# Moving one tile's gated sum from VectorE to GpSimd in the second joint block of a transformer kernel

## The reference

```python
for i in range(DEPTH):                      # DEPTH = 2
    h = _modulate(_rmsnorm(x, g_attn[i]), sh_a, sc_a)
    hc = _modulate(_rmsnorm(xc, g_attn[i]), shc_a, scc_a)
    q, k, v = _split_qkv(h, w_qkv[i])
    qc, kc, vc = _split_qkv(hc, w_qkv[i])
    ...                                     # joint attention, w_o, gates
    y = _hier_moe(tokens, ...)              # two experts of 32 per token, weighted sum
    x = x + gt_f * y[:b * n].reshape(b, n, d)
    if not last:
        xc = xc + gtc_f * y[b * n:].reshape(xc.shape)
```

## Time and profile before

| | us |
|---|---|
| median of 3 runs | 2367.75 |
| the runs | 2365.62, 2367.75, 2369.81 |
| profiled execution, device time | 2365.99 |
| its span in the trace | 2364.2 |
| busy: PE / DVE / ACT / POOL | 2154.2 / 1110.1 / 688.3 / 199.9 |

### The profile page before, as it was taken

How to read it: one execution, slowest core, us unless ns; L and a number is a source line. 1 busy time by engine, 2 the same in 40 slices (tenths; PEclk the granted TensorE clock), 3 DMA queues, 4 the chain that set the end, 5 groups by cost and what they waited for, 6 DMA issues and landing times.

```text
span 2364.2 us, 28723 instructions
## 1 busy us (share of the span) xinstructions
PE 2154.2 (91%) x11290; PEld 1348.1 (57%) x11290; DVE 1110.1 (47%) x1761; ACT 688.3 (29%) x1100; POOL 199.9 (8%) x304
## 2 busy tenths in 40 slices
PE   7999999998899999988988888888789999999996
PEld 5778788876787888865833233333466533333332
DVE  6677655465676556568531111111687422222223
ACT  4243344345234443257211111111337111111110
POOL 2000000010000000100111111011120000000000
PEclk9989999999899999999879899899999899999998
DMA  9745576573755656520779999999850699999995
GB/s 304 267 146 187 194 246 205 171 266 138 245 186 187 224 173 227 180 49 6 293 292 419 426 427 427 427 427 425 327 157 21 240 413 427 427 427 428 428 427 232
DMA packets 174936, 657.04 MB, mean 278 GB/s; under 512 B 15991, under 2 KB 61639, under 8 KB 149472
## 3 DMA queue, kind: packets, MB, share of 16 engines
q1 hardware_dynamic: 159216, 622.65, 68.1%
q0 software_dynamic: 13776, 29.99, 3.8%
q10 hardware_dynamic: 1824, 2.73, 0.3%
HBM read 649.97 MB, written 23.79 MB: 285 GB/s over the span
## 4 chain that ended last, share of the span: by engine, by line
PE 59%; DMA 21%; DVE 13%; ACT 4%; issue 1%; POOL 1%; SPq 1%; ACTq 0%; POOLq 0%; DVEq 0%
PE bank L737 30%; DMA sb_ring<-in_w_up 16%; PE bank L1374 11%; PE bank L1399 5%; DMA sb_arena<-in_w_up 3%; DVE sb_ring_rounded L2024 2%; PE bank L1332 2%; PE bank L751 2%; ACT sb_hb L1615 1%; PE bank L773 1%; DVE sb_st L2228 1%; PE bank L1385 1%; PE bank L926 1%; ACT sb_ring_rounded L1510 1%; PE bank L940 1%
## 5 line engine op out<-in xcount | busy, mean ns | idle before, releaser
L737 PE MATMUL bank<-sb_ring_rounded,sb_hT_rounded 128*128 128x512 f32 x2432 | 603.3, 397 | 22.8 <-DVE sb_ring_rounded L2024 9.7
L737 PEld LDWEIGHTS bank<-sb_ring_rounded,sb_hT_rounded 128*128 128x128 f32 x2432 | 457.9, 190 | 122.2 <-issue 12.6
L1374 PE MATMUL bank<-sb_ring,sb_arena 128*64 128x512 f32 x1568 | 436.7, 638 | 72.7 <-DMA sb_ring<-in_w_up 64.7
L2024 DVE TENSOR_TENSOR sb_ring_rounded<-sb_ring,sb_ring_rounded 128x2048 fp32r<-128x2048 f32 (+1 forms) x142 | 315.1, 2260 | 109.3 <-ACT sb_ring_rounded L1510 104.8
L737 PE MATMUL bank<-sb_ring_rounded,sb_arena_rounded 128*128 128x512 f32 x1408 | 356.4, 395 | 8.2 <-DVE sb_arena_rounded L2011 7.6
L1510 ACT ACTIVATE sb_ring_rounded<-sb_ring 128x2048 fp32r<-128x2048 f32 x146 | 268.1, 1887 | 125.6 <-PE bank L737 100.7
L1374 PEld LDWEIGHTS bank<-sb_ring,sb_arena 128*64 128x64 f32 x1568 | 132.4, 146 | 300.3 <-issue 296.0
L737 PEld LDWEIGHTS bank<-sb_ring_rounded,sb_arena_rounded 128*128 128x128 f32 x1408 | 265.8, 190 | 63.6 <-DVE sb_arena_rounded L2011 7.9
L1907 ACT ACTIVATE sb_hb<-bank 64x512 f32<-64x512 f32 x64 | 37.8, 590 | 688.9 <-PE bank L1374 688.9
L1399 PE MATMUL bank<-sb_ring,sb_arena 128*64 128x512 f32 x768 | 174.8, 597 | 2.5 <-DVE sb_arena L2857 2.5
L2857 DVE COPY sb_arena<-bank 128x256 f32<-128x256 f32 x64 | 27.1, 424 | 310.6 <-PE bank L1385 310.5
(11 more groups left out here) (376 smaller groups left out, 2259.4 us busy)
## 6 DMA issues: line engine op xcount, KB each, us to landing
sb_ring<-in_w_gate SPq DMA_DIRECT2D x50, 2048.0 KB, 30.2
sb_ring<-in_w_up SPq DMA_DIRECT2D x48, 2048.0 KB, 30.6
sb_ring<-in_w_down SPq DMA_DIRECT2D x48, 2048.0 KB, 25.6
sb_ring<-in_w_ada SPq DMA_DIRECT2D x48, 1024.0 KB, 7.4
sb_ring<-in_ffn_w_gu SPq DMA_DIRECT2D x44, 1024.0 KB, 7.7
sb_ring<-in_xa_w_kv SPq DMA_DIRECT2D x16, 1024.0 KB, 7.4
sb_ring<-in_ffn_w_down SPq DMA_DIRECT2D x16, 1024.0 KB, 6.6
sb_hT<-in_w_up SPq DMA_DIRECT2D x8, 2048.0 KB, 30.5
```

The source lines that it names most:

```text
L737: ins = pe.matmul(bank[b][0:rows, :], rnd(x), rnd(w[:, k, :]), start=start and k == k0 and q == 0, stop=stop and k == k1 - 1 and q == len( ...
L1374: ins = pe.matmul(bank[2 * j + part][part * ROWS:(part + 1) * ROWS, :], mxT[:, j, k, :], w[:, k, :], start=k == 0, stop=k == KD - 1)
L2024: dve.tensor_tensor(rnd(w), w, whole(high_of(n)[:, k0:k1, :]), ALU.subtract).then_inc(*c.up(s["w_lo"]))
```

## The change

For tile 3 of the second joint block, ScalarE scales row 1 too, with its weight `mwt[:, 7:8]`, right after `scale_rows`. DVE's `combine(3, ctx_gate)` and the flag behind it are gone. GpSimd waits for the gate row and for the fifth `y_scaled` (both rows of tile 3 scaled), and does three 128x1024 operations, each waiting for the one before: sum of the two rows, times the gate, added to `xs[:, 3, :]`. They stand between its two `fill` calls and `norms()` for tiles 2 and 3. ScalarE's square of tile 3 waits for the new semaphore `last_rows_added` in place of DVE's flag.

```diff
@@ ScalarE, joint(1)
                     norm([1])
                     scale_rows([2, 3])
+                    act.activation(rows_of(3)[:, 1, :], rows_of(3)[:, 1, :], ACT.Copy, scale=mwt[:, 7:8]).then_inc(*c.up(s["y_scaled"]))
...
-                        act.wait_ge(*c.next(s["act_go"]))
+                        act.wait_ge(*(c.next(s["act_go"]) if i == 0 else (s["last_rows_added"], 1)))
                         act.activation(hb[:, i, :], xs[:, 2 + i, :], ACT.Square, accum_out=st[:, i:i + 1]).then_inc(*c.up(s["act_back"]))
@@ DVE, joint(1)
                     project(0, 1, 1)
-                    combine(3, ctx_gate)
-                    settle()
-                    flag(s["act_go"])
                     mean_square(0)
@@ GpSimd
+        ctx_gate_loaded = 16 * 5
...
                 fill(1, mod(l, 1 - (l == 0), 0))
+                if l == 1:
+                    a, b = rows_of(3)[:, 0, :], rows_of(3)[:, 1, :]
+                    pool.wait_ge(s["bcx"], ctx_gate_loaded)
+                    pool.wait_ge(s["y_scaled"], 5)
+                    step(pool.tensor_tensor(a, a, b, ALU.add))
+                    step(pool.tensor_tensor(a, a, ctx_gate, ALU.mult))
+                    pool.tensor_tensor(xs[:, 3, :], xs[:, 3, :], a, ALU.add).then_inc(s["last_rows_added"], 1)
                 norms()
```

More of the change, by code:

```diff
@@ L184, in build_program @@
             "small_l", "small_loaded", "stat_ready", "stat_rstd", "w_used", "x_loaded",
-            "y_loaded0", "y_loaded1", "y_loaded2", "y_loaded3", "y_scaled", "y_stored", "weights_ready", "weights_stored", "weights_loaded", "y_zeroed", "own_rows", "own_w", "own_full", "w_hi", "w_lo", "x_hi", "p_ready", "bc0", "bc1", "bc2", "tok_stored0", "tok_stored1",
+            "y_loaded0", "y_loaded1", "y_loaded2", "y_loaded3", "y_scaled", "y_stored", "weights_ready", "weights_stored", "weights_loaded", "y_zeroed", "own_rows", "own_w", "last_rows_added", "own_full", "w_hi", "w_lo", "x_hi", "p_ready", "bc0", "bc1", "bc2", "tok_stored0", "tok_stored1",
         )}
```

## The result

| | before | after |
|---|---|---|
| median of 20 runs, us | 2367.17 | 2371.15 |
| lowest and highest, us | 2360.70 to 2371.75 | 2368.25 to 2376.46 |
| ratio of the times, 95% interval | | 1.0018 (1.0012 to 1.0024) |
| span of the profiled execution, us | 2364.2 | 2369.9 |

By the medians the change costs 4.0 us; by the ratio it costs 0.18%, with an interval of 2.8 to 5.7 us. The forecast was 2372.0, and +4.2 us.

A forecast was written before the change was run, and what follows sets the result against it. VectorE was taken to bound the second joint block, with ScalarE's rounding 1.88 us behind; delays of 1.6 and 4.5 us, less 1.9 of slack, gave +4.2 us on 2367.75: 2372.0 us, range 2367.0 to 2376.0.

The forecast's parts named there:

- Part 1: ScalarE's added scaling ahead of the rounding L1510: nothing hides it, so L2024 may start 1.04 us later.
- Part 2: Removing 4.2 us of VectorE's tile 3 work gains at most 1.88 us alone, as L1510 is then late.
- the slack of 1.88 us: At L2024 for `qkv1`+2: ScalarE's rounding was ready at 1721.94 us, VectorE took it at 1723.82.
- The 0.84 us: Best gain at L2024 for `qkv1`+2 if GpSimd's work cost the others nothing: start at 1722.98 for 1723.82.
- Part 3: GpSimd's three operations, about 2.4 us each, exclude VectorE; the flag behind `combine(2)` comes 6.1 us later.
- the sum: The flag behind `combine(2)` 6.1 us later, less 1.9 us of slack: L2024 for `qkv1`+2 comes 4.2 us later.
- the remainder of the first sum: GpSimd's first operation, mostly in VectorE's idle time: first L2024 delayed 1.6 us, with 1.04 from ScalarE's scaling inside.
- The rival with 3.66 us an operation: GpSimd's operations grow in proportion to size, 3.66 us each: +8.0 us, 2375.8; chance 0.13.
- The order of turns: A waiting GpSimd operation gets in at VectorE's next boundary; second and third lie before `combine(2)` ends: +4.5 us.
- The rival in which GpSimd loses its turns: GpSimd's second and third operations run only behind `combine(2)`, while VectorE waits anyway: +0.9 us, 2368.7; chance 0.08.
- the rival on the clock: TensorE idles longer and stays three us more at the lower clock, costing 1.5 us: +5.7, 2373.5; chance 0.1.
- Nothing later takes it back: Behind L2024 for `qkv1`+2 order is unchanged and expert weight loads shift too, so the whole 4.2 us remains.

The follow-up runs named there:

- e1: Kernel before plus only ScalarE's added scaling of row 1 of tile 3, VectorE still summing that tile; ratio 1.0010 (1.0000 to 1.0020).
- e3: Kernel before without VectorE's combine(3) and its flag, so that tile's expert rows are left out; ratio 0.9995 (0.9985 to 1.0005).
- e2: Changed kernel without GpSimd's three operations, so that tile's expert rows are left out; ratio 1.0004 (0.9994 to 1.0015).
- e7: Changed kernel with all three ScalarE scalings moved behind the rounding of `qkv1`+1; ratio 1.0004 (0.9994 to 1.0014).
- e4: Changed kernel with GpSimd's three operations on 512 of the 1024 elements; ratio 1.0007 (0.9997 to 1.0017).
- e8: e6 with the scratch zeroing issued behind the load of `qkv1`+2 and a TensorE filler product between turning tiles 2 and 3; ratio 0.9988 (0.9978 to 0.9998).
- e5: Kernel before with both context-tile scalings moved behind ScalarE's rounding of `qkv1`+1; ratio 0.9995 (0.9982 to 1.0009).
- e6: e5 with ScalarE squaring the queries of tile 0 in place of VectorE; ratio 0.9999 (0.9988 to 1.0011).
- e9: e5 with the scratch zeroing issued behind the load of `qkv1`+2, VectorE still summing tile 3; 2366.36 us, ratio 0.9998 (0.9988 to 1.0007).
- e10: e7 with the scratch zeroing issued behind the load of `qkv1`+2, GpSimd summing tile 3; 2365.60 us, ratio 0.9996 (0.9986 to 1.0005).

## Why the prediction was right

**Part 1** was sized right: 1.04 us forecast, VectorE's idle time 1.03 us longer, and 0.97 us at L2024 in e1.

**Part 2**, the slack of 1.88 us, was right as far as it went: e3 gained 1.89 us at L2024. The 0.84 us that it calls the best of this order was not reached in e2 (+0.21): the landing of the weights of `qkv1`+2, which the prediction leaves out, came last there. With the landing of before it would not have, so whether the 0.84 can be had stays open.

**Part 3**: the operation took 2.42 us (2.4 forecast). What each waiting one costs VectorE was 2.26 in the sum and measured 2.13 (3.41 - 1.28) in after and 2.07 in e7; the remainder of the first sum measured 7.29 - 4.49 - 2.13 = 0.67, with 0.54 forecast (1.58 less 1.04). The sum by the measured terms: 1.04 + 0.67 + 2 x 2.13 - 1.88 = 4.09, and 4.07 measured. The 0.67 is what the pair's stretch leaves when one hold of 2.13 is taken off, so of this sum only the one hold is measured by itself. The two errors, 0.13 us too little and 0.26 too much, cancelled in part. The rival with 3.66 us an operation fell with the 2.42.

The Trainium skill (SBUF — State Buffer, § SBUF: two separate sides) has the lock held for the whole instruction. The trace agrees that both sides block, but one sum held VectorE 2.13 us and not 2.42. About half of the difference is start-up, as forecast: L3220's bar ends 1723.95 - 1721.69 = 2.26 us after the VectorE operation that it waited for. The rest is that VectorE goes on 0.1 to 0.2 us before GpSimd's bar ends: L2963, with 1.28 us of work, ends at 1725.02. With 2.42 us a hold the sum of the measured terms would have been 0.6 us higher. For GpSimd's power operation the trace does not bear the rule out (the last section shows it), and the measurement decides.

**The order of turns** was as forecast: a waiting operation of either engine gets in at the next boundary, even between the two halves of the pair. The rival in which GpSimd loses its turns fell in after; half of it came true in e7, where one operation of GpSimd did slip behind `combine(2)` and cost nothing.

**Behind L2024** two things that the sum did not have cancelled. TensorE idled 3.18 us in place of 2.29 and then took 1747.11 - 1733.38 = 13.73 us for the two products, where it took 12.48 before: +1.25 us, the mechanism and near the size of the rival on the clock (1.5), which brings the turn to +5.31. But at tiles 2 and 3 it kept its clock, which it had partly lost before. The turn before and after, and the stretches of after:

```profile
1740.93 1.17 PE L773 MATMUL bank<-sb_cst,sb_hb 128*128 128x128 f32 x8 [1.16 <-DVE sb_arena_rounded L2011]
```

```profile
1749.29 1.16 PE L773 MATMUL bank<-sb_cst,sb_hb 128*128 128x128 f32 x8 [1.14 <-DVE sb_arena_rounded L2012]
```

```profile
1733.38:1737.00 3.62, 3.62 (x9) 2.85 (x10) 3.62 (x4) 1.05 (x4) 0.55 (x1) 0.50 1.07 219
...
1752.00:1765.00 13.00, 13.00 (x56) 10.10 (x57) 10.87 (x16) 4.47 (x5) 1.64 (x1) 1.00 0.00 0
```

1.00 from 1752 on, against 0.88 before over the same products, gave 1.34 us back: from the turn to the release 15.56 us in place of 16.90. So the +3.97 at the release is the sum of a right mechanism and two opposite turns of the clock; that the total came within 0.2 us of the forecast is partly luck. The runs e1 and e4, which lost the clock at other places, came out 0.2 and 1.2 us higher at the release than at L2024. Where each run loses it is read from its trace; why there is not shown.

**Nothing later takes it back**: the medians fit it, 4.0 us (2.8 to 5.7) against 3.97 at the release. The traces alone could not tell. From the release to the end before took 2364.2 - 1757.83 = 606.4 us and after 605.1, but the ten experiments lie between 603.0 and 608.6 without order.

## What to carry to other kernels

Moving elementwise work on two SBUF tiles from VectorE to GpSimd freed nothing while VectorE did such work itself: three moved operations of 1.25 us came back as 0.7 + 2 x 2.1 us of waiting. A moved sum cost nothing only where VectorE idled or worked without two SBUF inputs, as the third one in e7; that it would gain there no run shows. So read what VectorE does in the very stretch, not its busy share.

Before taking work from the engine that the chain names, measure how far behind it the next release lies, and the one behind that. Here ScalarE's rounding was 1.9 us behind, the landing of the weights close to that (in time in e3, 0.97 us late in e2), and TensorE's clock could take back what was left. Only the kernel that treated all of them (e8) has a time below that of before, and its interval leaves out 1 by little.

## What the runs showed of the hardware that was not expected

- GpSimd and VectorE take strict turns at instruction boundaries, also between two VectorE operations that are issued back to back with no wait between them but a semaphore already met (1717.2 and 1721.7 in after). A GpSimd bar of 4.33 us holds 2.4 us of work.
- GpSimd's power operation does not hold VectorE for its length. Of the two L3128 below the first took 3.96 us and the second 2.90. The first began beside VectorE's L2068, which ended at 1737.74, and its extra 1.06 us fit a wait for that. It ended at 1740.5, so it was at work when VectorE's L2601, with two inputs in SBUF, ran at 1739.23, and that took 0.29 us. L2569 of the same shape took 0.28 from 1756.9 on, with GpSimd idle. So what the sums cost VectorE can't be carried over to every GpSimd operation. Rows of before:

```profile
1736.56 6.85 POOL L3128 TENSOR_TENSOR sb_st<-sb_st,sb_cst 128x16 f32<-128x16 f32 x2 [1.27 <-DVE sb_st L2070]
...
1739.23 0.29 DVE L2601 TENSOR_TENSOR sb_bc<-sb_cst,sb_bc 128x128 f32<-128x128 f32 x1
```

- A VectorE copy from PSUM of 0.69 us was not stretched at all beside a GpSimd sum of two SBUF tiles (e7).
- Less work can mean a slower stretch: with 4.2 us less on VectorE (e3), TensorE idled 4.23 us, was granted 0.50 for the next 8 us, and the release came 1.97 us later in that trace.
- Whether the weights of `qkv1`+2 make ScalarE wait varies by us between the traces: no wait in before, after, e3 and e4, where they landed 19.8 to 21.6 us after their issue; 0.66 to 3.93 us in e1, e2, e5, e6 and e7, where they took 23.8 to 25.1 us; none in e8, e9 and e10 with the zeroing behind them, where they took 11.3 to 11.5 us. e1's wait of 0.76 us cost nothing, since VectorE was later still. What sets the landing inside the DMA queue was not separated further.
